# Four low parts of every gate/up chunk formed by accumulating transfers instead of VectorE, in a two-layer decoder trunk

## The chip, the core and the metric

The kernel runs on one core of one Trainium2 chip. The metric is the time of the whole program on the device in microseconds, so less is better. The core's engines run side by side and meet only at semaphores: TensorE (PE) multiplies, VectorE (DVE) and ScalarE (ACT) work elementwise, GpSimd (POOL) and SyncE (SP) here mostly start transfers (DMA).

## What is computed

A residual stream x of 256 tokens by 2048 channels, float32, goes through two layers. Each has a mixer (a gated spatial mixer in the first, attention in the second) and a feed forward part. The change lies in the feed forward parts alone:

```python
D_MODEL = 2048
SEQ = 256
D_FF = -(-8 * D_MODEL // (3 * 256)) * 256      # 5632
...
def swiglu_ffn(x, norm_g, w_gate, w_up, w_down):
    h = rms_norm(x, norm_g)
    return (jax.nn.silu(h @ w_gate) * (h @ w_up)) @ w_down
...
        x = x + swiglu_ffn(x, ffn_norm[layer], ffn_w_gate[layer], ffn_w_up[layer], ffn_w_down[layer])
```

## The kernel before

**Two parts for each number.** TensorE multiplies in a reduced float format (fp32r). So every float32 weight is split into a high part (rounded to that format) and a low part (what is left), and the activations too; a product is three matmuls: high with high, low with high, high with low (`products`, lines 1609 to 1611). All of them have 512 columns. Each weight tile is loaded from HBM into `raw`, ACT writes the high part (`w_hi`, line 741), DVE the low part as raw minus high (`w_lo`, line 1160), and TensorE uses both.

**Chunks, half groups, pairs.** The 5632 hidden columns of a layer are eleven chunks of 512, c = 0 to 10. A chunk needs the products of the activations with 2048 rows of the gate weights (g) and as many of the up weights (u). The rows are cut in eight steps of 256, numbered 0 to 7. Steps 4 to 7 of g and u are plain: one such step is a **half group**, 12 matmuls (`plain_group`). Steps 0 to 3 are done for g and u together as **pairs** s0 to s3, in a form that needs seven block products, 21 matmuls, where two half groups need 24 (`pair`). A pair asks more of DVE: three sums from the raw tile (`pair_sums`, lines 1149, 1152, 1155), and three low parts (`pair_lo`, lines 1165, 1168, 1171) behind three high parts of ACT (`pair_hi`, line 730). Chunk 0 of a layer has an order of its own ("first"); the other ten are of kind "chunk". Behind chunks 3, 7 and 10 comes the down projection of the hidden columns made so far ("down" blocks), with half groups and pairs of the same kind.

**What sets the order.** No scheduler: every engine's order is written by hand as a list of such items, and semaphores alone hold the engines together. For a "chunk" PE and DVE go in the order of `ORDERS`, ACT by a list of its own:

```python
"chunk": items("g4 g5 g6 s0 g7 s1 u4 s2 u5 s3 u6 u7"),
...
    ACT_ORDERS = {"chunk": items("g4 g5 g6 g7 s0 s1 u4 s2 u5 s3 u6 u7")}
```

Between the items each engine does what belongs to the chunk before: ACT reads one bank behind g5 (line 764), applies silu behind g6 (line 770) and writes the high part of the hidden tile behind s0 (line 609); DVE sums the banks behind g5 (lines 1183 to 1191) and behind g6 (1200, 1207), then makes the sums of s0; behind s0 comes the hidden tile's low part (983), behind g7, u4 and u5 the sums of s1, s2 and s3. PE transposes the hidden tile behind g5 (line 1516).

**Buffers.** `w_hi` and `w_lo` are rings of four half groups: ACT may write half group m when PE has used half group m - 4. A pair has one buffer, of which each third is written again when PE has used it (`s_used`). `raw` has four slots of two half groups or one pair; the loads of a chunk are g4 g5, g6 g7, s0, s1, u4 u5, s2, s3, u6 u7, and SP starts a load when every reader of what the slot held is done (`slot_free`), in this order.

**The way that the table ADDED switches.** The code has a second way to make a low part. For a half group named in `ADDED`, ACT writes the high part and then, with a second instruction, minus the high part into `w_lo` (line 743); POOL starts a transfer that adds the raw tile onto it (`add_raw`, line 541), 512 KB, from SBUF to SBUF, and PE waits for its landing (`lo_added`) in place of DVE's signal. The raw slot is free for the next load when that transfer has landed. In the kernel before, `ADDED` is empty for every kind of block, so no instruction of this way is issued.

```python
                ins = nc.scalar.activation(w_hi[:, m % RING, :, :], src, ACT.Copy)
                if m in ADDED_HG:
                    nc.scalar.activation(w_lo[:, m % RING, :, :], src, ACT.Copy, scale=-1.0).then_inc(neg_ready, 1)
...
                        pool.dma_start(w_lo[:, m % RING, :, :].bitcast(F32), raw[:, slot, half * HG:(half + 1) * HG, :],
                                       accum_op=ALU.add).then_inc(lo_added[m % RING], 16)
```

The functions that read the changed tables, with their line numbers in the profile:

Of the kernel before, what the change touches and what calls it, by code (L numbers as in the profile page):

```python
# [49 lines left out]
def yoco_kernel(nc, x, a_norm, a_w_in, a_ln_g, a_ln_b, a_w_s, a_b_s, a_w_out, kv_norm, w_k, w_v, k_norm,  # L50
# [27 lines left out]
    def items(text):  # L78
        return [(w[0], int(w[1:])) for w in text.split()]
# [16 lines left out]

    ADDED = {"chunk": [], "first": [], "down 0": [], "down 1": [], "down middle": []}


    ACT_ORDERS = {"chunk": items("g4 g5 g6 g7 s0 s1 u4 s2 u5 s3 u6 u7")}

    def kind(k):

        if k[1] == "chunk":
            return "chunk" if k[2] else "first"
        return f"down {k[3]}"

    def order(k):  # L110
        return ORDERS[kind(k)]

    def loads(k):
        return LOADS[kind(k)]
# [15 lines left out]
    for layer in range(2):  # L130
        reads = SLOT_READ[layer]
        reads += [[("half group", hg - 6 + 2 * n)] for n in range(RAW)]
        for p, (c0, c1) in enumerate(PARTS):
# [5 lines left out]
            for k in blocks:  # L139
# [11 lines left out]
                for item in order(k):  # L151
# [3 lines left out]
                    else:  # L155
                        HG_OF[k, item] = hg
                        if item in ADDED[kind(k)]:
                            ADDED_HG.append(hg)
                        hg += 1
                LAST_PAIR[k], END_OF[k] = n_pair - 1, hg  # L160
                for load in loads(k):
                    slot = len(reads) % RAW
                    n_both[slot] += len({m for m, _ in load}) > 1 or load[0][0] == "s"
                    for item in load:
                        LOAD_OF[k, item], BOTH_OF[k, item] = len(reads) - RAW, n_both[slot]
                    reads.append([("pair", PAIR_OF[k, item[1]] + 1) if item[0] == "s" else
                                  ("added", HG_OF[k, item]) if item in ADDED[kind(k)] else
                                  ("half group", HG_OF[k, item] + 1) for item in load])
# [22 lines left out]
    def in_slot(load):  # L191

        return load % RAW, load // RAW + 1
# [22 lines left out]
    with ExitStack() as ctx:  # L216
# [274 lines left out]
        def _(pool):  # L491
# [40 lines left out]
            def add_raw(layer):  # L532
                for k in (k for k in NUMBER if k[0] == layer):
                    for item in order(k):
                        if item not in ADDED[kind(k)]:
                            continue
# [22 lines left out]
        def _(act):  # L559
# [197 lines left out]
            def feed_forward(layer, norm, last_save, last_lhs):  # L757
# [18 lines left out]
                def block_hi(k, hooks):  # L776
                    for item in ACT_ORDERS.get(kind(k), order(k)):
                        slot, count = in_slot(LOAD_OF[k, item])
                        both = BOTH_OF[k, item]
                        if item[0] == "s":  # L780
                            pair_hi(PAIR_OF[k, item[1]], slot, both, before + count)
                        else:
                            load, = [w for w in loads(k) if item in w]
                            half = load.index(item)
                            if half == 0 and load[1][0] != item[0]:
                                plain_hi(HG_OF[k, item], slot, half, s_landed[slot], both)
                            else:
                                plain_hi(HG_OF[k, item], slot, half, raw_landed[slot], before + count)
                        for work in hooks.get(item, ()):
                            work()  # L790
# [158 lines left out]
        def _(dve):  # L949
# [213 lines left out]
            def pair_lo(n, slot):  # L1163
                dve.wait_ge(s_cast, n * 3 + 1)
                nc.vector.tensor_tensor(s_lo[:, 0:3, :], raw[:, slot, 1:4, :], s_hi[:, 0:3, :].bitcast(F32), ALU.subtract)\  # L1165
                    .then_inc(blocks_split, 1)
                dve.wait_ge(s_cast, n * 3 + 2)
                nc.vector.tensor_tensor(s_lo[:, 5:7, :], sums_b[:, 2:4, :], s_hi[:, 5:7, :].bitcast(F32), ALU.subtract)\  # L1168
                    .then_inc(t24_split, 1)
                dve.wait_ge(s_cast, n * 3 + 3)  # L1170
                nc.vector.tensor_tensor(s_lo[:, 3:5, :], sums_b[:, 0:2, :], s_hi[:, 3:5, :].bitcast(F32), ALU.subtract)\  # L1171
                    .then_inc(s_split, 1)

            def feed_forward(layer, norm, first_hooks):
# [74 lines left out]
                def block_lo(k, hooks):  # L1249
                    for item in order(k):  # L1250
                        slot, _ = in_slot(LOAD_OF[k, item])
                        if item[0] == "s":
                            pair_lo(PAIR_OF[k, item[1]], slot)
                        elif item not in ADDED[kind(k)]:
                            load, = [w for w in loads(k) if item in w]
# [616 lines left out]
```

## Time and profile before

| | |
|---|---|
| time, median of 3 runs | 2097.47 us (2097.42 to 2097.56) |
| the profiled execution, its own time | 2096.73 us |
| its span in the profile | 2094.6 us |
| TensorE busy | 2076.8 us, 99% of the span |
| VectorE busy | 1731.5 us, 83% |
| ScalarE busy | 1150.4 us, 55% |
| GpSimd busy | 41.9 us, 2% |
| TensorE clock granted | 1.00 |
| HBM read | 399.56 MB, 192 GB/s over the span |

The ends of matmuls are modelled in this profile, and a matmul is put down as 389 ns though the next one starts 227 ns behind it. So PE can look busy while it loses up to some 160 ns between two matmuls. Its losses are read from the starts in the timeline, from the idle time of its weight loads (PEld), and from the length of equal pieces of the program.

### The profile page before, as it was taken

The page shows a single profiled execution, that of the slowest core. Times are in us where ns is not written, and L with a number is a line of the kernel's source. Part 1 is how long each engine was busy: PE and PEld are TensorE (multiplying, and loading weights), DVE is VectorE, ACT ScalarE, POOL GpSimd, SP SyncE. Part 2 cuts the span into 40 slices and gives each one's busy share as a digit, 9 for nine tenths or more (in the row PEclk, how much of TensorE's full clock was granted, in tenths as well). Part 3 has the DMA queues.
Part 4 walks back from the last instruction along what each step waited for, and adds up shares of the span by engine and source line. Part 5 has one row for each costly group of instructions (what it writes and reads, how often), then busy time and mean ns, then how long its engine had stood idle before and what let it go on. Part 6 is the DMA issues. An engine that isn't in the chain of part 4 may idle for free.

```text
span 2094.6 us, 24421 instructions
## 1 busy us (share of the span) xinstructions
PE 2076.8 (99%) x9394; PEld 1709.2 (82%) x9394; DVE 1731.5 (83%) x1907; ACT 1150.4 (55%) x1392; POOL 41.9 (2%) x47
## 2 busy tenths in 40 slices
PE   9999999999999999999999999999999999999999
PEld 8888888888888888888888888878888888888887
DVE  5466579999899998998566666589999899988997
ACT  6444555555455554556666655465555455554553
POOL 1000000000000000000011001000000000000000
PEclk9999999999999999999999999999999999999999
DMA  8655545656465664555554454545556464665554
GB/s 327 207 174 177 181 155 208 220 187 215 160 223 181 215 209 173 207 181 202 198 184 162 159 181 166 173 154 203 209 199 205 171 224 166 221 216 175 193 191 151
DMA packets 203614, 403.19 MB, mean 192 GB/s; under 512 B 8080, under 2 KB 8688, under 8 KB 203248
## 3 DMA queue, kind: packets, MB, share of 16 engines
q1 hardware_dynamic: 202720, 398.50, 55.1%
q0 software_dynamic: 784, 3.19, 0.4%
q8 instruction: 74, 1.21, 0.2%
q14 instruction: 36, 0.29, 0.0%
HBM read 399.56 MB, written 2.10 MB: 192 GB/s over the span
## 4 chain that ended last, share of the span: by engine, by line
PE 63%; DVE 33%; issue 3%; ACT 1%; DMA 0%; SPq 0%; DVEq 0%; ACTq 0%
PE acc L1468 10%; PE acc L1472 10%; PE acc L1470 10%; PE acc L1609 9%; PE acc L1610 9%; PE acc L1611 9%; DVE w_lo L1160 6%; DVE s_lo L1165 5%; DVE sums_b L1149 4%; DVE s_lo L1168 3%; DVE sums_b L1152 2%; DVE sums_b L1155 2%; DVE s_lo L1171 2%; DVE sums_b L1191 1%; DVE stage L1187 1%
## 5 line engine op out<-in xcount | busy, mean ns | idle before, releaser
L741 ACT ACTIVATE w_hi<-raw 128x1024 fp32r<-128x1024 f32 x320 | 326.5, 1051 | 165.4 <-PE acc L1611 151.0
L1160 DVE TENSOR_TENSOR w_lo<-raw,w_hi 128x1024 fp32r<-128x1024 f32 x320 | 380.8, 1217 | 21.2 <-ACT w_hi L741 21.2
L730 ACT ACTIVATE s_hi<-sums_b 128x1024 fp32r<-128x1024 f32 x208 | 209.4, 1053 | 236.5 <-DVE sums_b L1155 235.6
L1609 PE MATMUL acc<-w_hi,a_hi 128*128 128x512 f32 x736 | 288.1, 391 | 1.3 <-DVE w_lo L1160 1.3
L1611 PE MATMUL acc<-w_hi,a_lo 128*128 128x512 f32 x736 | 286.6, 389 | 0.0
L1610 PE MATMUL acc<-w_lo,a_hi 128*128 128x512 f32 x736 | 286.4, 389 | 0.0
L1468 PE MATMUL acc<-w_hi,a_hi 128*128 128x512 f32 x640 | 254.6, 398 | 0.4 <-DVE a_lo L987 0.4
L961 DVE TENSOR_TENSOR w_lo<-raw,w_hi 128x1024 fp32r<-128x1024 f32 x127 | 154.8, 1236 | 116.7 <-ACT w_hi L579 116.6
L1472 PE MATMUL acc<-w_hi,a_lo 128*128 128x512 f32 x640 | 249.6, 390 | 0.0
L1470 PE MATMUL acc<-w_lo,a_hi 128*128 128x512 f32 x640 | 249.2, 389 | 0.0
L730 ACT ACTIVATE s_hi<-raw 128x1536 fp32r<-128x1536 f32 x104 | 154.6, 1486 | 114.1 <-PE acc L1611 114.1
L965 DVE SCALAR_TENSOR_TENSOR w_lo<-raw,gains,w_hi 128x512 fp32r<-128x512 f32 x192 | 134.4, 747 | 83.9 <-ACT w_hi L583 83.8
L579 ACT ACTIVATE w_hi<-raw 128x1024 fp32r<-128x1024 f32 x127 | 132.2, 1058 | 117.5 <-PE acc L1472 115.7
L1165 DVE TENSOR_TENSOR s_lo<-raw,s_hi 128x1536 fp32r<-128x1536 f32 x104 | 182.1, 1751 | 2.2 <-ACT s_hi L730 2.2
L1609 PE MATMUL acc<-w_hi,h_hi 128*128 128x512 f32 x448 | 174.7, 390 | 0.0
L1611 PE MATMUL acc<-w_hi,h_lo 128*128 128x512 f32 x448 | 174.3, 389 | 0.0
L1610 PE MATMUL acc<-w_lo,h_hi 128*128 128x512 f32 x448 | 174.3, 389 | 0.0
L1609 PEld LDWEIGHTS acc<-w_hi,a_hi 128*128 128x128 f32 x736 | 138.2, 188 | 29.7 <-issue 1.7
L1611 PEld LDWEIGHTS acc<-w_hi,a_lo 128*128 128x128 f32 x736 | 138.1, 188 | 28.9
L1610 PEld LDWEIGHTS acc<-w_lo,a_hi 128*128 128x128 f32 x736 | 138.2, 188 | 28.1
L583 ACT ACTIVATE w_hi<-raw,gains 128x512 fp32r<-128x512 f32 x192 | 126.2, 714 | 60.5 <-PE acc L1472 60.4
L1472 PEld LDWEIGHTS acc<-w_hi,a_lo 128*128 128x128 f32 x640 | 120.1, 188 | 25.6
(223 smaller groups left out, 3793.8 us busy)
## 6 DMA issues: line engine op xcount, KB each, us to landing
raw<-in_ffn_w_down_dram SPq DMA_DIRECT2D x68, 1024.0 KB, 5.0
raw<-in_ffn_w_gate_dram SPq DMA_DIRECT2D x46, 1024.0 KB, 5.8
raw<-in_ffn_w_up_dram SPq DMA_DIRECT2D x46, 1024.0 KB, 5.0
raw<-in_ffn_w_gate_dram SPq DMA_DIRECT2D x84, 512.0 KB, 3.8
raw<-in_ffn_w_up_dram SPq DMA_DIRECT2D x84, 512.0 KB, 5.1
raw<-in_a_w_in_dram SPq DMA_DIRECT2D x30, 1024.0 KB, 5.3
raw<-in_ffn_w_down_dram SPq DMA_DIRECT2D x40, 512.0 KB, 4.8
raw<-in_a_w_out_dram SPq DMA_DIRECT2D x16, 1024.0 KB, 4.9
```

Of the source, the lines that this page charges most:

```text
L730: nc.scalar.activation(s_hi[:, operands, :], src, ACT.Copy).then_inc(s_cast, 1)
L741: ins = nc.scalar.activation(w_hi[:, m % RING, :, :], src, ACT.Copy)
L961: nc.vector.tensor_tensor(lo, src, hi, ALU.subtract).then_inc(lo_split, 1)
L965: ins = nc.vector.scalar_tensor_tensor(out=lo[:, k, :], in0=src[:, k, :], scalar=gains[:, gain + kb:gain + kb + 1], in1=hi[:, k, :], op0=A ...
L1160: nc.vector.tensor_tensor(w_lo[:, m % RING, :, :], raw[:, slot, half * HG:(half + 1) * HG, :], w_hi[:, m % RING, :, :].bitcast(F32), ALU.s ...
L1165: nc.vector.tensor_tensor(s_lo[:, 0:3, :], raw[:, slot, 1:4, :], s_hi[:, 0:3, :].bitcast(F32), ALU.subtract)\
L1468: nc.tensor.matmul(acc[s][t][:, :], hi[:, kb, tok], w_hi[:, slot, k, :], start=kb == 0, stop=False)
L1470: nc.tensor.matmul(acc[s][t][:, :], hi[:, kb, tok], w_lo[:, slot, k, :], start=False, stop=False)
L1472: ins = nc.tensor.matmul(acc[s][t][:, :], lo[:, kb, tok], w_hi[:, slot, k, :], start=False, stop=kb == HG * n - 1)
L1609: nc.tensor.matmul(bank[:, :], hi, rhs_hi, start=start, stop=False)
L1610: nc.tensor.matmul(bank[:, :], hi, rhs_lo, start=False, stop=False)
L1611: return nc.tensor.matmul(bank[:, :], lo, rhs_hi, start=False, stop=stop)
```

## The change

Two tables change and nothing else. In a block of kind "chunk" (chunks 1 to 10 of both layers, 20 blocks) the half groups g7, u4, u5 and u7 get their low parts by the accumulating transfer. ACT's order moves too: u4 and u5 each stand one pair earlier, u7 stands ahead of s3, and u6 is last.

```diff
-    ADDED = {"chunk": [], "first": [], "down 0": [], "down 1": [], "down middle": []}
+    ADDED = {"chunk": items("g7 u4 u5 u7"), "first": [], "down 0": [], "down 1": [], "down middle": []}
...
-    ACT_ORDERS = {"chunk": items("g4 g5 g6 g7 s0 s1 u4 s2 u5 s3 u6 u7")}
+    ACT_ORDERS = {"chunk": items("g4 g5 g6 g7 s0 u4 s1 u5 s2 u7 s3 u6")}
```

The orders of PE and SP are the same row for row. On ACT, from g7 (the high part that follows the silu) to the first part of s1, before:

```order
L770 ACTIVATE stage<-stage,rstd 128x512 x2
L741 ACTIVATE w_hi<-raw 128x1024
L730 ACTIVATE s_hi<-raw 128x1536
L730 ACTIVATE s_hi<-sums_b 128x1024 x2
L609 ACTIVATE h_hi<-tr 128x512 x2
L730 ACTIVATE s_hi<-raw 128x1536
```

and now:

```order
L770 ACTIVATE stage<-stage,rstd 128x512 x2
L741 ACTIVATE w_hi<-raw 128x1024
L743 ACTIVATE w_lo<-raw 128x1024
L730 ACTIVATE s_hi<-raw 128x1536
L730 ACTIVATE s_hi<-sums_b 128x1024 x2
L609 ACTIVATE h_hi<-tr 128x512 x2
L741 ACTIVATE w_hi<-raw 128x1024
L743 ACTIVATE w_lo<-raw 128x1024
L730 ACTIVATE s_hi<-raw 128x1536
```

So g7 has a second write behind it, and the two of u4 stand between the hidden tile and s1. On DVE, from the hidden tile's low part to the sums of s2, before:

```order
L983 TENSOR_TENSOR h_lo<-tr,h_hi 128x512 x2
L1160 TENSOR_TENSOR w_lo<-raw,w_hi 128x1024
L1149 TENSOR_TENSOR sums_b<-raw 128x1024
L1152 TENSOR_TENSOR sums_b<-sums_b,raw 128x512
L1155 TENSOR_TENSOR sums_b<-sums_b,raw 128x512
L1165 TENSOR_TENSOR s_lo<-raw,s_hi 128x1536
L1168 TENSOR_TENSOR s_lo<-sums_b,s_hi 128x1024
L1171 TENSOR_TENSOR s_lo<-sums_b,s_hi 128x1024
L1160 TENSOR_TENSOR w_lo<-raw,w_hi 128x1024
L1149 TENSOR_TENSOR sums_b<-raw 128x1024
```

and now:

```order
L983 TENSOR_TENSOR h_lo<-tr,h_hi 128x512 x2
L1149 TENSOR_TENSOR sums_b<-raw 128x1024
L1152 TENSOR_TENSOR sums_b<-sums_b,raw 128x512
L1155 TENSOR_TENSOR sums_b<-sums_b,raw 128x512
L1165 TENSOR_TENSOR s_lo<-raw,s_hi 128x1536
L1168 TENSOR_TENSOR s_lo<-sums_b,s_hi 128x1024
L1171 TENSOR_TENSOR s_lo<-sums_b,s_hi 128x1024
L1149 TENSOR_TENSOR sums_b<-raw 128x1024
```

The low parts of g7 and u4 are gone from DVE, and those of u5 and u7 further on. POOL, which issued nothing in the chunks, gets one run of transfers for each layer:

```order
L541 DMA w_lo<-raw 128x1024 x40
```

It stands between the small norm steps of the two layers; nothing else was or is due on POOL inside the chunks.

## Rows read from the trace of the kernel before

**Rows 1.** Page, part 1: busy us, share of the span, count of instructions

```profile
PE 2076.8 (99%) x9394; PEld 1709.2 (82%) x9394; DVE 1731.5 (83%) x1907; ACT 1150.4 (55%) x1392; POOL 41.9 (2%) x47
```

**Rows 2.** Windows from transpose to transpose, layer 0: into chunks 2, 3 and down

```profile
core 0: us, PE busy (x) PEld busy (x) DVE busy (x) ACT busy (x) POOL busy (x), PEclk, DMA share, GB/s
336.80:378.73 41.93, 41.93 (x190) 34.48 (x189) 41.45 (x41) 24.50 (x25) 0.00 (x0) 1.00 0.58 201
378.73:421.60 42.87, 42.34 (x189) 34.38 (x188) 42.36 (x42) 24.50 (x25) 0.00 (x0) 1.00 0.56 196
421.60:464.47 42.87, 42.38 (x190) 34.39 (x189) 42.42 (x42) 24.19 (x25) 0.00 (x0) 1.00 0.56 196
```

**Rows 3.** Waits of the weight loads, whole span: us in total, times, longest

```profile
PEld acc L1609 <- DVE s_lo L1165: 29.2, 57, 1.1
```

**Rows 4.** Timeline of PE, chunk 6 of layer 0, into s1 and s2 (start, length)

```profile
602.78 0.39 PE L1611 MATMUL acc<-w_hi,a_lo 128*128 128x512 f32 x1
603.64 0.50 PE L1609 MATMUL acc<-s_hi,a_hi 128*128 128x512 f32 x1 [0.47 <-DVE s_lo L1165]
603.98 0.40 PE L1610 MATMUL acc<-s_lo,a_hi 128*128 128x512 f32 x1
...
611.03 0.39 PE L1611 MATMUL acc<-w_hi,a_lo 128*128 128x512 f32 x1
611.30 0.50 PE L1609 MATMUL acc<-s_hi,a_hi 128*128 128x512 f32 x1
611.64 0.39 PE L1610 MATMUL acc<-s_lo,a_hi 128*128 128x512 f32 x1
```

**Rows 5.** Timeline of PE, chunk 4 (the one behind a down block), into s1

```profile
559.65 0.39 PE L1611 MATMUL acc<-w_hi,a_lo 128*128 128x512 f32 x1
560.76 0.50 PE L1609 MATMUL acc<-s_hi,a_hi 128*128 128x512 f32 x1 [0.73 <-DVE s_lo L1165]
```

**Rows 6.** Timeline of DVE, chunk 6: g7, sums and low part of s1, then on

```profile
598.11 1.22 DVE L1160 TENSOR_TENSOR w_lo<-raw,w_hi 128x1024 fp32r<-128x1024 f32 x1
599.24 1.22 DVE L1149 TENSOR_TENSOR sums_b<-raw 128x1024 f32<-128x1024 f32 x1
...
601.84 1.75 DVE L1165 TENSOR_TENSOR s_lo<-raw,s_hi 128x1536 fp32r<-128x1536 f32 x1
...
606.91 1.21 DVE L1149 TENSOR_TENSOR sums_b<-raw 128x1024 f32<-128x1024 f32 x1
...
621.10 4.62 DVE L1160 TENSOR_TENSOR w_lo<-raw,w_hi 128x1024 fp32r<-128x1024 f32 x4
```

**Rows 7.** Timeline of ACT, chunk 6 and the start of chunk 7

```profile
595.01 1.06 ACT L609 ACTIVATE h_hi<-tr 128x512 fp32r<-128x512 f32 x2
597.85 1.49 ACT L730 ACTIVATE s_hi<-raw 128x1536 fp32r<-128x1536 f32 x1 [1.78 <-PE acc L1611]
...
624.06 0.60 ACT L764 ACTIVATE sums_b<-acc 128x512 f32<-128x512 f32 x1 [0.98 <-PE tr L1611]
...
629.58 1.04 ACT L741 ACTIVATE w_hi<-raw 128x1024 fp32r<-128x1024 f32 x1
```

**Rows 8.** Timeline of SP, chunk 6: the load of u6 u7

```profile
605.89 0.37 SPq L428 DMA_DIRECT2D raw<-in_ffn_w_up_dram  x1
```

**Rows 9.** Page, part 6: transfers, KB each, median us from issue to landing

```profile
raw<-in_ffn_w_up_dram SPq DMA_DIRECT2D x46, 1024.0 KB, 5.0
raw<-in_ffn_w_gate_dram SPq DMA_DIRECT2D x84, 512.0 KB, 3.8
```

**Rows 10.** The same view over the first 60 us: POOL's large transfers

```profile
w_s_nat<-in_a_w_s_dram POOLq DMA_DIRECT2D x1, 1024.0 KB, 8.2
...
ln_bias<-in_a_ln_b_dram POOLq DMA_DIRECT2D x1, 1024.0 KB, 13.8
```

**Rows 11.** Timeline of POOL: how long the issues took it

```profile
37.09 1.25 POOL L514 DMA_DIRECT2D w_s_nat<-in_a_w_s_dram  x1
38.35 0.56 POOL L515 DMA_DIRECT2D ln_gain<-in_a_ln_g_dram  x1
```

## The prediction, made before the changed kernel had run

> **What bounds the kernel now.** I read the page's first part, then the windows chunk by chunk, then the timeline where PE loses time. PE is busy 99% of the span, DVE 83% [rows 1]: at first sight TensorE is the bound and relief on DVE is worth nothing. The windows say where that is not so. From transpose to transpose a chunk takes 42.87 us, in which DVE is busy for 42.36 and 42.42 us, while the piece into chunk 2, with the same work of PE and DVE a little ahead, takes 41.93 [rows 2]. ACT has 24.5 us of work in it. So inside the chunks DVE is as full as PE, and PE waits for it a little.
>
> How: PE's weight loads waited for line 1165, the first low part of a pair, 57 times, 29.2 us [rows 3] (that sum holds the usual gaps between loads too, so it is not yet the loss). Of the 57, 54 are three (s1, s2, s3) in each of 18 chunks; chunk 1 of the two layers has the other three. Two matmuls normally start 227 ns apart. Into s1 of chunk 6 they start at 602.78 and 603.64, 0.63 us late, and the next only at 603.98, 0.11 us late again, as its weights could not be loaded ahead. Into s2 the two losses are 0.27 - 0.227 = 0.04 and 0.34 - 0.227 = 0.11 [rows 4], into s3 the same. Why 0.04 each time: between s1 and s2 DVE's own round, from one L1149 to the next, is 606.91 - 599.24 = 7.67 us [rows 6], and PE's is 21 + 12 matmuls of 227 ns, 7.48. PE is held back to DVE's pace.
>
> **What the change removes.** The loss in a usual chunk is 0.63 + 0.11 + 2 x 0.15 = 1.04 by rows 4; by the windows it is 42.87 - 41.93 = 0.94, plus the one wait of about 0.15 that chunk 1 has itself, 1.09 [rows 2]. I take 1.07. In a chunk behind a down block the wait into s1 is 560.76 - 559.65 - 0.23 = 0.88 [rows 5], so 1.3 in all. Sum: 14 x 1.07 + 4 x 1.3 + 3 x 0.15 = 15.0 + 5.2 + 0.4 = 20.6 us.
>
> DVE is rid of four instructions of 1.22 us in a chunk, started 1.13 us apart (598.11 and 599.24 in rows 6): 4 x 1.13 = 4.5 us of DVE, against a loss of about 1.1. Over 20 chunks that is 80 instructions and 90 us off DVE. Is it off at the right place? For s1, yes twice. g7's low part stands directly ahead of the sums of s1, so these and the low part behind them come 1.13 us sooner. And DVE starts the chunk's bank sums sooner: now a run of four low parts ends at 625.72 [rows 6], although ACT's read of the bank, which they also need, is done at 624.66 [rows 7]. With u7 gone they follow ACT, some 0.9 us sooner. s1 was 0.63 late and would be 1.4 us early. Behind a down block only the first of the two helps: 0.88 late becomes 0.25 early. For s2 and s3 DVE's round falls to 7.67 - 1.13 = 6.5 us against PE's 7.48, so its lead grows. All four gaps close, and the 0.11 behind each with them. What is late next is nothing within a microsecond in a usual chunk: PE runs at its own pace.
>
> **What it adds on ACT.** Four more writes (minus the high part), each about as w_hi, 1.04 us [rows 7]: 4.2 us onto 24.5 of 42.87 [rows 2]. Where each lies: g7's second write stands ahead of s0's high parts, which end up waiting for DVE's sums anyway. The two of u4 now stand between the hidden tile, done at 596.07, and s1: they end at about 598.1, where s1's first part now starts at 597.85, released by PE [rows 7]. That costs 0.3 us at most, out of the 1.4. u5 lies likewise between s1 and s2, where ACT idled about as long as before. u7 ahead of s3 needs its load landed: SP issues u6 u7 at 605.89 [rows 8], behind DVE's last part of s1, and 1 MB lands 5.0 us later [rows 9], at 610.9, or 2 us sooner if s1 is. s2's high parts on ACT are done at about 609. So ACT may idle there until 610 or so, and u7's pair ends near 612; s3's first part is due when PE has used a third of s2, near 613. No cost. u6, last, is done long before PE's turn.
>
> **What it adds in transfers.** 4 x 512 KB in a chunk, each issued when ACT's second write is done. The deadline is PE's turn for that half group. The nearest is u4: ready at 598.1, used when PE has gone through s1, 603.0 + 4.76 = 607.8, so 9.7 us ahead. For g7 it is about 11.6 us, for u5 and u7 over 11. The trace of before has no accumulating transfer. From below: a plain load of 512 KB lands after 3.8 us [rows 9]. From above: POOL's own transfers, twice as large, at a time when the DMA engines were nearly full, landed after 8.2 us and, the third in a row, after 13.8 [rows 10]. Issuing took POOL 0.56 to 1.25 us [rows 11], four times in 42 us. I take 6 us, an estimate between 3.8 and 8.2 since one is issued alone and is half as large: hidden, with 3 us to spare. The raw slots stay held until the landing, but this too is earlier than now: g7's slot is free at about 595 instead of behind DVE's g7 at 599.33. DMA load: the chunk's own weights keep the engines busy for a share of 0.56 at 196 GB/s, 8.4 MB [rows 2]; 2.1 MB more is 0.14, twice that if the add reads its target as well: 0.70 to 0.84. There is room, with less of it.
>
> **Sum.** 20.6 removed, 0 added: 2096.73 - 20.6 = 2076.1 for the profiled execution. The median of the three runs lies 0.74 above it, so 2076.9.
>
> **Rivals.** (1) *POOL and DVE share a way into SBUF.* If a transfer's issue holds DVE up for its 0.56 to 1.25 us [rows 11], four of them take 2.2 to 5.0 us from DVE, against 4.5 given: at the upper end nothing is gained, about 2097; at the lower end all is still gained. For it: DVE has hardly a gap in which POOL could go unseen. Against it: POOL reads no tile in an issue, and three issues near 38 us disturbed nothing that I can see. The Trainium skill, "SBUF — State Buffer", section "SBUF: two separate sides", has a rule that speaks against this change: a VectorE operation with two SBUF inputs excludes a GpSimd operation that reads SBUF, for the whole instruction, and whoever comes first holds it. All of DVE's low parts have two SBUF inputs. By it the time would be this rival's 2097 if it held for an issue, and POOL's issue would itself start up to 1.75 us late; no run shows it for a transfer that is only issued.
>
> (2) *The accumulating transfer is slow* (the one that ends slower). If landing takes L us, u4 is late by L - 9.7, in 20 chunks, while 20.6 is won. The sides are even at L = 10.7. At 13.8, the slowest that POOL's transfers showed [rows 10], it is 4.1 x 20 - 20.6 = 61 us slower, 2158. For it: adding reads twice and writes once, and four such transfers share the engines with loads that come in bursts. Against it: half the size of those in rows 10, and alone in the queue.
>
> (3) *A part only.* Loads crowded by the adds land later, so ACT writes u7 and then s3 late, or the chunks behind a down block keep their waits since only 0.25 us is to spare there. With one wait of 0.3 to 0.5 us left in each chunk, 6 to 10 us stay: 2083 to 2087.
>
> (4) *The tables move nothing*: excluded, as the built order shows DVE without the rows.
>
> **How the numbers follow.** Full gain, 2075 to 2079: 0.62. Part, 2079 to 2092: 0.17. No gain by rival 1, 2093 to 2101: 0.07. Slower by rival 2: 0.14. The range runs from 2075.0 (the sum with the losses taken 10% higher) to 2098.0, and leaves out rival 2 with little else. 0.2% is 4.2 us, about what a measurement of this kernel can tell from no change. Faster 0.79, same 0.07, slower 0.14.
>
> **What would show it.** Right: PE's weight loads no longer wait for line 1165, a chunk from transpose to transpose is 41.8 us in all 20, DVE shows idle time in the chunks, some 4 us each, ahead of the bank sums and of the pairs, and L1160 counts 240 in place of 320. The landing of w_lo<-raw is 4 to 8 us. Wrong: PE waits for w_lo<-raw by DMA ahead of u4 (rival 2), DVE's 1.22 and 1.75 us grow or gaps open while POOL issues (rival 1), or PE waits stay at s3 or behind down blocks (rival 3). A landing above 9.7 us alone would overturn the sign.

## The result: 2105.4 us, slower by 0.37%

| | before | changed |
|---|---|---|
| median, 20 runs each | 2097.43 us | 2105.37 us |
| lowest to highest | 2097.05 to 2098.55 | 2097.48 to 2112.85 (19 runs) |
| ratio to before, 95% interval | | 1.0037 (1.0028 to 1.0045) |
| profiled execution, its span | 2094.6 us | 2100.8 us |

The forecast was 2076.9, 20.6 us faster. One of the 20 runs of the changed kernel took 5993 us; there is no trace of it, the comparison leaves it out, and nothing below explains it. The others spread over 15 us where before they spread over 1.5. The traced run took 2102.49 us, so it shows a little less than the usual loss.

Page of the changed kernel, part 1 and part 3 (queue, packets, MB, share of 16 engines), against [rows 1]:

```profile
PE 2075.0 (99%) x9394; PEld 1711.9 (81%) x9394; DVE 1648.5 (78%) x1827; ACT 1223.2 (58%) x1472; POOL 110.5 (5%) x127
...
q1 hardware_dynamic: 202720, 398.50, 57.1%
q0 software_dynamic: 12304, 45.14, 10.5%
```

DVE is rid of 83 us and 80 instructions (90 us were forecast), ACT has 73 us more (84). The chunks, again from transpose to transpose, the same pieces as in [rows 2], and further on the pieces into chunk 7 and into the down block behind it:

```profile
core 0: us, PE busy (x) PEld busy (x) DVE busy (x) ACT busy (x) POOL busy (x), PEclk, DMA share, GB/s
336.86:379.55 42.69, 42.02 (x190) 34.53 (x189) 38.27 (x38) 28.18 (x29) 3.46 (x4) 1.00 0.89 251
379.55:422.60 43.05, 42.01 (x190) 34.53 (x189) 38.28 (x38) 28.18 (x29) 3.44 (x4) 1.00 0.83 244
422.60:464.33 41.73, 41.73 (x190) 34.62 (x189) 37.46 (x37) 27.15 (x28) 2.59 (x3) 1.00 0.83 244
...
633.82:676.63 42.81, 42.44 (x190) 34.34 (x189) 38.18 (x38) 28.06 (x29) 3.44 (x4) 1.00 0.84 246
676.63:720.23 43.60, 42.46 (x190) 34.36 (x189) 38.21 (x38) 26.68 (x28) 2.59 (x3) 1.00 0.82 237
```

The forecast was 41.8 us for each. Of the 16 such pieces of the trace two have 41.7; six, of 42.1 to 42.8, keep a part of the gain; eight are longer than before. The worst one, from 1991.5 us on, takes 46.19 in place of 42.87. DVE now has 2.8 to 7.6 us without work in each, so DVE's pace is no longer the matter. Who waits for whom (us in total, times, longest), against [rows 3]:

```profile
ACT w_hi L741 <- DMA raw<-in_ffn_w_gate_dram: 57.3, 16, 6.6
ACT w_hi L741 <- DMA raw<-in_ffn_w_up_dram: 51.7, 20, 5.9
...
PEld acc L1609 <- DVE stage L1187: 12.6, 10, 2.7
PEld acc L1609 <- DVE s_lo L1165: 11.6, 14, 2.6
```

The 54 regular waits of PE for DVE are gone. In their place ACT waits for weight loads, 36 times for 109 us, where the kernel before waited 2.3 us in all for such loads; and PE waits 24 times, for up to 2.7 us: ahead of g4 for DVE's bank sums (L1187) and ahead of a pair for its low part (L1165). PE waits for a landing of `w_lo<-raw` by itself only 0.2 us in the whole span, so the deadline that the prediction watched is met. The transfers (KB each, median us from issue to landing), against [rows 9]:

```profile
raw<-in_ffn_w_gate_dram SPq DMA_DIRECT2D x46, 1024.0 KB, 8.1
raw<-in_ffn_w_up_dram SPq DMA_DIRECT2D x46, 1024.0 KB, 6.5
...
w_lo<-raw POOLq DMA_DIRECT2D x80, 512.0 KB, 8.6
```

The loss has two places in a chunk. **Place 1**, chunk 2 of layer 0, into s3. Timelines of SP, POOL, ACT, DVE and PE:

```profile
391.45 0.37 SPq L428 DMA_DIRECT2D raw<-in_ffn_w_up_dram  x1
...
391.72 0.85 POOL L541 DMA_DIRECT2D w_lo<-raw  x1 [5.90 <-ACT w_lo L743]
...
401.53 1.06 ACT L741 ACTIVATE w_hi<-raw 128x1024 fp32r<-128x1024 f32 x1 [4.91 <-DMA raw<-in_ffn_w_up_dram]
402.50 1.04 ACT L743 ACTIVATE w_lo<-raw 128x1024 fp32r<-128x1024 f32 x1
403.44 1.47 ACT L730 ACTIVATE s_hi<-raw 128x1536 fp32r<-128x1536 f32 x1
...
404.95 1.76 DVE L1165 TENSOR_TENSOR s_lo<-raw,s_hi 128x1536 fp32r<-128x1536 f32 x1 [3.77 <-ACT s_hi L730]
...
405.33 0.39 PE L1611 MATMUL acc<-w_hi,a_lo 128*128 128x512 f32 x1
406.76 0.50 PE L1609 MATMUL acc<-s_hi,a_hi 128*128 128x512 f32 x1 [1.04 <-DVE s_lo L1165]
```

SP issues the load of u6 u7, and 0.3 us later POOL issues the transfer of u5. The load needs 10.1 us, where in the same chunk of the kernel before it needed 4.9. ACT stands at u7, which the new order puts ahead of s3, so s3 is late on ACT, then on DVE, then on PE, by 1.2 us. In the trace this load needs 9.7 to 10.7 us in five of the 20 chunks, and PE is late by 0.8 us or more at s3 in just these five; in the other 15 it lands after 6.1 to 7.6 us although u5's transfer follows it as closely. The five differ from the rest in u4's transfer: there it still had 2.6 us or more to its landing when the load was issued (here it landed at 394.06), elsewhere 2.1 us or less. The two go together in the trace; that the one is the cause of the other is not shown.

**Place 2**, from the end of chunk 4 to that of chunk 5. (The prediction and its rows call the stretch from 590 to 625 us chunk 6. It is chunk 5: its s1 starts at 603.64, one chunk of 42.88 us behind the 560.76 of chunk 4.) The chain that released each step (start, length):

```profile
561.96 8.43 DMA w_lo<-raw
570.46 9.35 DMA raw<-in_ffn_w_gate_dram
579.83 1.07 ACT w_hi L741
...
584.64 1.24 DVE stage L1187
...
604.22 0.95 ACT w_lo L743
605.17 0.28 issue
605.46 8.66 DMA w_lo<-raw
614.15 0.03 issue
614.18 7.90 DMA raw<-in_ffn_w_gate_dram
```

and what PE lost by it:

```profile
585.92 0.50 PE L1609 MATMUL acc<-w_hi,a_hi 128*128 128x512 f32 x1 [0.91 <-DVE stage L1187]
```

The transfer of u5 lands after 8.43 us; only then is the raw slot of u4 u5 free, and only then does SP load g4 g5 of the next chunk, with g6 g7 in line behind. POOL has just issued u7's transfer (570.23). The load takes 9.35 us. ACT then has to write g4 and g5, DVE their low parts, and the bank sums come behind these in DVE's order, so PE starts g4 of chunk 5 1.1 us late (the matmul ahead of it starts at 584.63). In the kernel before SP issued this load later, at 571.85, but it landed after 5.6 us.

The chain then goes on through DVE and ACT to u5's transfer of chunk 5, and PE is no part of it. So it is a **loop**, and its length is the pace of the chunks as soon as it is longer than PE's own 41.7 us. From the landing of the load of g4 g5 to the issue of the next u5 transfer it takes 25.7 us in ten of the 14 chunks that follow another chunk (27.4 to 28.4 in the four behind a chunk that lost time at place 1); 0.06 us lie between u5's landing and the load. The next round is 25.7 + 8.66 + 7.90 = 42.3 us, and from 605.46 to the next u5 transfer, at 647.73, it is just that. PE stays in front only if the landing of u5's transfer and the load behind it together need less than 41.7 - 25.7 = 16.0 us; in the change they need 15.1 to 19.2, in the median 16.8. In 14 of the 20 chunks the chain that ended last goes through u5's transfer.

### The profile page after: what moved, and what is told of

It reads as the page before. It is cut to its first block, busy times and chain, and to the rows that moved or that the text cites. A ratio compares the mean times of both kernels' runs of the same rounds, so it can differ in the third digit from the quotient of the medians.

```text
span 2100.8 us, 24501 instructions
## 1 busy us (share of the span) xinstructions
PE 2075.0 (99%) x9394; PEld 1711.9 (81%) x9394; DVE 1648.5 (78%) x1827; ACT 1223.2 (58%) x1472; POOL 110.5 (5%) x127
## 3 DMA queue, kind: packets, MB, share of 16 engines
q0 software_dynamic: 12304, 45.14, 10.5%
## 4 chain that ended last, share of the span: by engine, by line
PE 62%; DVE 17%; DMA 14%; ACT 4%; issue 3%; SPq 0%; DVEq 0%; ACTq 0%
PE acc L1468 10%; PE acc L1472 10%; PE acc L1470 10%; PE acc L1609 9%; PE acc L1611 8%; PE acc L1610 8%; DMA w_lo<-raw 6%; DMA raw<-in_ffn_w_gate_dram 4%; DVE s_lo L1165 2%; DVE sums_b L1149 2%; DMA raw<-in_ffn_w_down_dram 2%; DVE w_lo L1160 2%; DMA raw<-in_ffn_w_up_dram 1%; ACT w_hi L741 1%; DVE stage L1187 1%
## 5 line engine op out<-in xcount | busy, mean ns | idle before, releaser
L1160 DVE TENSOR_TENSOR w_lo<-raw,w_hi 128x1024 fp32r<-128x1024 f32 x240 | 286.6, 1219 | 76.6 <-ACT w_hi L741 76.3
L1609 PE MATMUL acc<-w_hi,a_hi 128*128 128x512 f32 x736 | 289.0, 393 | 8.8 <-DVE stage L1187 7.3
L1611 PE MATMUL acc<-w_hi,a_lo 128*128 128x512 f32 x736 | 286.7, 390 | 0.0
L961 DVE TENSOR_TENSOR w_lo<-raw,w_hi 128x1024 fp32r<-128x1024 f32 x127 | 154.8, 1236 | 116.6 <-ACT w_hi L579 116.5
L1165 DVE TENSOR_TENSOR s_lo<-raw,s_hi 128x1536 fp32r<-128x1536 f32 x104 | 182.3, 1753 | 32.5 <-ACT s_hi L730 32.5
L1609 PE MATMUL acc<-w_hi,h_hi 128*128 128x512 f32 x448 | 175.1, 391 | 1.3 <-DVE stage L1187 1.1
L1611 PE MATMUL acc<-w_hi,h_lo 128*128 128x512 f32 x448 | 174.4, 389 | 0.0
L1609 PEld LDWEIGHTS acc<-w_hi,a_hi 128*128 128x128 f32 x736 | 138.2, 188 | 40.3 <-DVE stage L1187 10.0
L1611 PEld LDWEIGHTS acc<-w_hi,a_lo 128*128 128x128 f32 x736 | 138.1, 188 | 29.0
```

The costliest lines, as they stand in the source:

```text
L961: nc.vector.tensor_tensor(lo, src, hi, ALU.subtract).then_inc(lo_split, 1)
L1160: nc.vector.tensor_tensor(w_lo[:, m % RING, :, :], raw[:, slot, half * HG:(half + 1) * HG, :], w_hi[:, m % RING, :, :].bitcast(F32), ALU.s ...
L1609: nc.tensor.matmul(bank[:, :], hi, rhs_hi, start=start, stop=False)
L1611: return nc.tensor.matmul(bank[:, :], lo, rhs_hi, start=False, stop=stop)
```

## Experiments

All runs have a comparison with the kernel before on the same chip, of 2097.2 to 2097.7 us. Where the edit is to the changed kernel, the diff is against it.

### Is it the transfers at all? Without them, and with small ones

```diff
-                        pool.dma_start(w_lo[...], raw[...], accum_op=ALU.add).then_inc(lo_added[m % RING], 16)
+                        continue
...
-                        sp.wait_ge(lo_added[count % RING], 16 * n_added(count))
+                        sp.wait_ge(neg_ready, n_neg(count))
```

(and PE in the same way)

> The changed kernel with its 80 accumulating transfers left out: ACT still writes minus the high part into w_lo, and PE and the raw slots wait for that write instead of a landing (so these low parts stay without their raw half; everything else is computed). Theory A, the transfers' bytes crowd the DMA engines and the weight loads land late: all new stalls go with them, 1 MB loads land in 5 to 6 us again, and the predicted gain appears, 2075 to 2079 us. Theory B, ACT's second writes and its new order hold up the pairs: most of the loss stays, 2095 to 2110. Theory C, POOL's issues disturb DVE: as A, since the issues go too.

2074.51 us, ratio 0.9892 (0.9875 to 0.9908).

```diff
-                        pool.dma_start(w_lo[:, m % RING, :, :].bitcast(F32), raw[:, slot, half * HG:(half + 1) * HG, :],
+                        pool.dma_start(w_lo[:, m % RING, 0, 0:P].bitcast(F32), raw[:, slot, half * HG, 0:P],
```

> The changed kernel with each accumulating transfer cut to the first 128 of the 1024 columns, 64 KB in place of 512 (so only these columns get the raw part added). Issues, waits and semaphores are all still there. Theory A (bytes crowd the loads): loads land in 5 to 6 us, 2075 to 2080 us. Theory C (the issues themselves, or the mere chain of ACT write, POOL issue, landing, raw slot free) : half or more of the loss stays, above 2088.

2074.37 us, 0.9892 (0.9875 to 0.9908). So the relief of DVE is worth 22.7 us, ACT's second writes and its order cost nothing, and neither do 80 issues on POOL, which take it 0.86 us each at this size as at the full one: with theories B and C gone, rival 1 of the prediction falls. DVE's instructions are as long as before also in the changed kernel, 1219 and 1753 ns against 1217 and 1751. So nothing of the exclusion between VectorE and GpSimd that the Trainium skill describes ("SBUF — State Buffer", section "SBUF: two separate sides") was to be seen for transfers that POOL only issues.

### Bytes beside the loads, or the held slot?

In this kernel the four transfers keep their size, but read `w_hi`, so the raw slots are free as soon as ACT has written.

```diff
-                        pool.dma_start(w_lo[:, m % RING, :, :].bitcast(F32), raw[:, slot, half * HG:(half + 1) * HG, :],
+                        pool.dma_start(w_lo[:, m % RING, :, :].bitcast(F32), w_hi[:, m % RING, :, :].bitcast(F32),
...
-                        sp.wait_ge(lo_added[count % RING], 16 * n_added(count))
+                        sp.wait_ge(neg_ready, n_neg(count))
```

> All four transfers with all their 512 KB, but each adds from w_hi of the same half group instead of from raw (so these low parts are wrong: minus high plus high), and SP therefore frees the raw slot as soon as ACT has written, not at the landing. PE still waits for the landing. Theory A (bytes crowd the loads): loads still land late, 2095 to 2110 us. Theory D (what hurts is that the raw slot is held 8.6 us until the transfer lands, so the next load starts late): 2074 to 2080.

2075.26 us, 0.9896 (0.9879 to 0.9912), and this with transfers as slow and loads of g slower still:

```profile
raw<-in_ffn_w_gate_dram SPq DMA_DIRECT2D x46, 1024.0 KB, 10.0
raw<-in_ffn_w_up_dram SPq DMA_DIRECT2D x46, 1024.0 KB, 6.5
...
w_lo<-w_hi POOLq DMA_DIRECT2D x80, 512.0 KB, 8.5
```

Theory A alone, which I had held first, is refuted: loads that take 10 us do no harm if they are issued early enough. SP's timeline shows by how much: the load of g4 g5 behind chunk 2 is issued right behind that of u6 u7, at 391.28, where the changed kernel issues it at 402.21. The raw slot that is held until the landing matters. Place 1 is gone too: the load of u6 u7 lands after 5.1 to 7.5 us here, though u5's transfer runs beside it and u7 stands ahead of s3. But a held slot alone is not it either:

### Shorter transfers that still hold their slots

```diff
-                                       accum_op=ALU.add).then_inc(lo_added[m % RING], 16)
+                                       ).then_inc(lo_added[m % RING], 16)
```

> All four transfers, same source, target and bytes, but plain copies instead of adds (so w_lo holds the raw values). A packet of 4096 bytes takes 328 ns as an add and 171 to 174 ns in POOL's plain transfers. If the time that the add keeps an engine is what crowds the loads: landing falls from 8.6 to 5 to 7 us, and the kernel to 2076 to 2090. If only the number of bytes or the path through POOL counts: as the change, 2098 to 2110.

2074.36 us, 0.9891 (0.9874 to 0.9907). Page, part 3:

```profile
q0 software_dynamic: 12304, 45.14, 5.4%
```

And the 80 transfers by their destination, `w_lo`:

```profile
DMA to landing us min/median/max: 2.8/6.7/8.9
```

The same packets and bytes as plain copies take 5.4% of the engines' time in place of 10.5%; less 0.4% for the other transfers of that queue, 5.0 against 10.1: **an adding transfer keeps the engines twice as long as a copying one.** The landing falls from 8.6 to 6.7 us in the median, and the load of g4 g5 behind it lands after 5.8 us in place of 8.2. In the loop of place 2 the two together need 12.7 us in place of 16.8: under the 16.0 that PE leaves, and the loss is gone.

```diff
-                        pool.dma_start(w_lo[:, m % RING, :, :].bitcast(F32), raw[:, slot, half * HG:(half + 1) * HG, :],
+                        pool.dma_start(w_lo[:, m % RING, 0, :].bitcast(F32), raw[:, slot, half * HG, :],
```

> All four transfers, each cut to its first half, 256 KB (so half of the columns' low parts stay without their raw part). Theory A (crowding by engine time): landing about 5 to 6.5 us, PE waits nearly gone, 2074 to 2082 us, as the slack is some 2 us. If the loss went with the bytes in proportion, it would be halfway: about 2088.

2074.70 us, 0.9892 (0.9875 to 0.9908), landing 6.7 us too, landing and load together 12.6. The loss is not in proportion to the bytes: it begins where the loop becomes longer than PE's work, and the changed kernel, with 16.8 against 16.0, lies just past that. This fits its spread from run to run, but only one run of it is traced.

### Which slot, which transfer

u5's transfer alone reads `w_hi` and frees its slot early:

```diff
+                    elif what == "added" and ADDED_HG.index(count) % 4 == 2:
+                        sp.wait_ge(neg_ready, n_neg(count))
                     elif what == "added":
...
+                        src = w_hi[:, m % RING, :, :].bitcast(F32) if item == ("u", 5) else \
+                            raw[:, slot, half * HG:(half + 1) * HG, :]
```

> The changed kernel, but the transfer of u5 alone adds from w_hi in place of raw, full size (so u5's low part is wrong), and the raw slot of u4 u5 is free as soon as u4's transfer has landed and ACT has written u5. All transfers run with all their bytes. Theory D1 (u5's landing holds the slot into which g4 g5 of the next chunk must be loaded, and g6 g7 queue behind it on SP): most of the 30 us come back, 2075 to 2082. Theory D2 (the loss needs u7's or g7's slot): 2095 to 2108.

2081.39 us (2078.75 to 2082.22), 0.992 (0.9904 to 0.9937). u5's slot is out of the loop; the waits for L1187, place 2, are gone, and place 1 is what is left:

```profile
PEld acc L1613 <- DVE s_lo L1169: 7.9, 6, 2.2
...
ACT w_hi L745 <- DMA raw<-in_ffn_w_up_dram: 52.3, 20, 5.6
ACT w_hi L745 <- DMA raw<-in_ffn_w_gate_dram: 3.2, 2, 1.6
```

(The edit adds four lines, so L1169 here is L1165 elsewhere.) The same edit for u7, index 3 in place of 2:

> The same for u7 alone: its transfer adds from w_hi, full size, and its raw slot is free as soon as ACT has written. Theory D1: as the change, 2098 to 2110, since u5 still holds its slot. Theory D2: 2075 to 2085.

2105.00 us (2101.62 to 2109.92, 9 runs), 1.0034 (1.0024 to 1.0044): as the change. It is u5's slot, then, and not u7's. Yet u5's transfer in its slot does no harm when u7 has none:

```diff
-    ADDED = {"chunk": items("g7 u4 u5 u7"), ...}
+    ADDED = {"chunk": items("g7 u4 u5"), ...}
...
-    ACT_ORDERS = {"chunk": items("g4 g5 g6 g7 s0 u4 s1 u5 s2 u7 s3 u6")}
+    ACT_ORDERS = {"chunk": items("g4 g5 g6 g7 s0 u4 s1 u5 s2 s3 u6 u7")}
```

> Three transfers, g7, u4, u5; u7's low part on DVE again and u7 last on ACT. Theory D1: u5 still holds its slot, but no transfer of u7 shares the engines with the loads of g4 g5 and g6 g7: a good part of the loss stays, 2080 to 2100. If only four at once are too many: 2074 to 2077.

2074.33 us, 0.9892 (0.9876 to 0.9909). My expectation leaned to the loss staying; it did not. u5's transfer lands as late as in the change (8.8 us in the median), but the load behind it now lands after 5.2: together 14.2 in this trace, under 16.0. With g7, u4 and u7 instead, in the order of the change:

> Three transfers, g7, u4, u7; u5's low part on DVE, ACT's order as in the change. Theory D1: no transfer holds the slot of u4 u5 late, so 2074 to 2080 although three transfers run. If the load of u6 u7 ahead of s3 on ACT is what hurts: 2085 to 2105.

2075.77 us, 0.9896 (0.9879 to 0.9912). Here u7 stands ahead of s3 too, but the load of u6 u7 lands after 5.1 us in the median and 6.9 at most, as no transfer of u5 runs beside it. So place 1 needs u5's transfer and u7's place ahead of s3; the run whose transfers read `w_hi` had both and no place 1, so the two alone do not make it.

### Bytes of u7, or its place in ACT's order

u7's transfer cut to 64 KB, the rest as in the change:

```diff
+                        part = (slice(0, 1), slice(0, P)) if item == ("u", 7) else (slice(0, HG), slice(0, CH))
...
```

> The change with the transfer of u7 alone cut to 64 KB (so most of u7's low part stays without its raw half); the other three full, ACT's order as in the change. If the loss has two places, (1) u5's transfer delays the load of u6 u7, for which ACT waits ahead of s3, and (2) u7's transfer delays the loads of g4 g5 that u5's held slot has already made late: place 1 stays and place 2 goes, 2079 to 2084. If place 2 is u5's held slot alone: 2095 to 2108. If both places need u7's bytes: 2074 to 2076.

2081.78 us (2080.67 to 2087.23), 0.9932 (0.9916 to 0.9949): place 2 is gone, place 1 is there with 7.9 us in 6 waits, as in the run with u5's slot freed early. So place 2 takes both: u5's slot freed late, and u7's bytes beside the loads that follow. Without these the load of g4 g5 lands after 5.9 us, and the two terms of the loop need 14.8. The same with u7 behind s3:

> The same, with u7 behind s3 in ACT's order, so nothing on ACT waits for the load of u6 u7 ahead of s3. By the two places neither is left: 2074 to 2076. If the order matters for nothing: as the run with u7 small in the change's order.

2079.72 us (2078.35 to 2081.65), 0.9913 (0.9896 to 0.9929), not the 2074 to 2076 that I expected. Place 1 is gone, as said, but a third one opens, in the waits of PE's weight loads (the edit adds two lines, so L1611 here is L1609 elsewhere):

```profile
PEld acc L1611 <- DMA w_lo<-raw: 8.3, 10, 1.5
```

Behind s3, u7's transfer is issued so late that PE waits for its landing, even at 64 KB. At full size this is the largest loss of all:

```diff
-    ACT_ORDERS = {"chunk": items("g4 g5 g6 g7 s0 u4 s1 u5 s2 u7 s3 u6")}
+    ACT_ORDERS = {"chunk": items("g4 g5 g6 g7 s0 u4 s1 u5 s2 s3 u6 u7")}
```

> All four transfers as in the change, but ACT takes u7 and u6 behind s3 in the old order, so a late load of u6 u7 no longer stands ahead of s3. Theory A1, the waits into s3 come from that place on ACT: they vanish, those ahead of the next chunk stay or grow by up to 1 us, since u7's transfer is now issued some 3 us later: 2088 to 2100 us. If the load itself is what counts wherever it stands: about as the change, 2102 to 2108.

2131.75 us (2123.45 to 2132.77), 1.0154 (1.0132 to 1.0176). The same row of the same view:

```profile
PEld acc L1609 <- DMA w_lo<-raw: 45.5, 20, 4.7
```

I had reckoned with 2088 to 2100, since I did not price u7's own deadline. The granted clock was 0.993 over this span, by which an estimated 15 of the 57 us above the run without transfers are PE at a lower clock, not waits. Beside u5's transfer u7 cannot win: ahead of s3 ACT waits for its load, behind s3 PE waits for its transfer. Without u5's it costs little, 2075.77 against 2074.35 with g7 and u4 alone (below).

### How much relief does DVE need?

```diff
-    ADDED = {"chunk": items("g7 u4 u5 u7"), ...}
+    ADDED = {"chunk": items("g7"), ...}
...
-    ACT_ORDERS = {"chunk": items("g4 g5 g6 g7 s0 u4 s1 u5 s2 u7 s3 u6")}
+    ACT_ORDERS = {"chunk": items("g4 g5 g6 g7 s0 s1 u4 s2 u5 s3 u6 u7")}
```

> Only g7 by an accumulating transfer, ACT in its old order. DVE is relieved of 1.13 us directly ahead of s1, where it was 0.65 us late, and its later rounds of 7.67 against 7.48 lose 0.2 us each twice, so s1 to s3 are just in time in a usual chunk and s3 or s1 a little late behind a down block. One transfer of 512 KB in a chunk, at its start. Theory A: few bytes, little crowding, 2077 to 2084 us. Theory C (issues disturb DVE by about a microsecond each): no gain, 2093 to 2098.

2075.77 us, 0.9898 (0.9881 to 0.9914). One transfer in a chunk brings nearly all, and the waits that stay are small:

```profile
PEld acc L1609 <- DVE s_lo L1165: 2.9, 12, 0.3
```

> Two transfers of 512 KB in a chunk, g7 and u4, ACT's order with u4 ahead of s1 and the rest as before. DVE is relieved of 2.3 us in a chunk. Theory A: two transfers 9 us apart early in the chunk, where only the loads of s2 and s3 are under way, crowd little: 2074 to 2078, at most 1.5 us better than g7 alone since the waits left there are 1.2 us. If every further transfer costs PE, it is slower than g7 alone, 2079 to 2090.

2074.35 us (2074.18 to 2074.66), 0.9890 (0.9874 to 0.9907). ACT's order there is "g4 g5 g6 g7 s0 u4 s1 s2 u5 s3 u6 u7". All chunks but the first are now as PE alone makes them, and DVE is still full, only no longer late:

```profile
336.80:378.50 41.70, 41.70 (x189) 34.63 (x189) 40.38 (x40) 26.39 (x27) 1.72 (x2) 1.00 0.76 232
378.50:420.20 41.70, 41.70 (x189) 34.59 (x188) 40.34 (x40) 26.40 (x27) 1.72 (x2) 1.00 0.72 226
```

This version beats both kernels: 1.1% faster than before, 31 us faster than the change, and level with the run that has no transfers at all (2074.51). The third transfer adds nothing to it (2074.33 with u5), the fourth costs 31 us.

## Why the prediction was wrong, point by point

- **The bound, right.** PE waits for DVE in the chunks, and the waits end when DVE is relieved. The sum was 20.6 us; without transfers 22.7 came back (2097.22 - 2074.51). 10% was missing: a usual chunk gives 1.17 us where I had 1.07. 41.8 us for a chunk was forecast, 41.70 measured.
- **ACT's added writes, right as to their own time** (nothing). The order was half right. "u7 ahead of s3 needs its load landed ... 1 MB lands 5.0 us later ... No cost": the load was issued as said, and landed after 10.1 us in the chunk shown, and after 6.1 or more in all, because u5's transfer runs beside it. I used the landing of a trace in which no transfer of POOL's ran beside the loads. That is place 1, some 7 us: 2081.4 and 2081.8 in the two runs that have it alone, against 2074.4.
- **The landing of the adding transfer: 6 us estimated, 8.6 measured** (4.4 to 10.4), above the 8.2 that I had as the upper end for it. PE's deadline of 9.7 us held all the same (u4's slowest landing took 9.7), so rival 2 as I priced it did not decide. As copies the same transfers landed in 6.7 us. The size was wrong since an add takes twice the engines' time of a copy; this I had left open in the engines' share (0.70 to 0.84; 0.82 to 0.89 in the pieces shown), but not in the landing.
- **The step that failed** is "hidden, with 3 us to spare. The raw slots stay held until the landing, but this too is earlier than now: g7's slot is free at about 595". It put the held slots at nothing, and it asked only when a slot is free, for one slot of three, and not how long the load behind it takes. For g7's slot it is true. The slot of u4 u5 was free at 605.46 + 8.66 = 614.1, hardly sooner than by DVE's old 614.66, and for a chunk that was to be a microsecond shorter; u7's transfer then slowed the load behind it (8.2 us in the median, 5.9 with u7 cut to 64 KB). That is place 2, about 23 us: the changed kernel's 2105 against 2081.4 with that slot free. Looking at this slot with my own numbers would not have shown it: with a landing of 6 us and a load of 5.0 the loop is 25.7 + 11.0 = 36.7 us, with 5 us to spare (an estimate from the change's own trace). Nor would either size alone: 8.8 + 5.0 and 6 + 8.2 (medians of the traced run) both stay below 16.0. It took the loop and both sizes as they were measured.
- **The rivals.** Rival 1 was refuted. Rival 3 named the mechanism, "loads crowded by the adds land later, so ACT writes u7 and then s3 late", and priced it at 6 to 10 us: right for place 1 (7). None of them has place 2: rival 3 stops at a part of the gain, and rival 2 has PE wait for the landing itself, which it did for 0.2 us in all. Rival 4 stayed excluded: L1160 counts 240. The range ended at 2098 because only rival 2 could make the kernel slower.

What stays open: the run of 5993 us; whether it is u4's transfer, still under way, that makes the load of u6 u7 need 10 us in some chunks and 6 to 8 in the others; and what sets the landing of u5's transfer and of the load behind it within their 15.1 to 19.2 us. The last decides which chunks lose at place 2, and no run varies it by itself.

## What to carry to other kernels

When work moves from an engine to transfers, list every buffer that the transfer holds until it lands, one by one, ask which load stands behind it, and follow that load on until the chain comes back to the same transfer of the next round: that loop has to be shorter than the round of the engine that you want to be the bound. Here an engine's read of the buffer ended in a microsecond, a transfer's in nine. Price the other loads at the landing they will have beside the new transfers, not at the one that they had without, above all where an in-order engine stands waiting for them ahead of something urgent. And relieve an engine by what it is late and not by what can be moved: here one of the four transfers gave 21.5 us, two 23, and all four lost 8.

## What the runs showed of the hardware that was not expected

An adding transfer within SBUF took twice the engine time of a copying one with the same packets and bytes (10.1% against 5.0% of 16 engines' span for 80 x 512 KB). The Trainium skill gives a fit for POOL's transfers, "DMA: Bandwidth & Descriptors", section "Anatomy of one DMA — SWDGE (gpsimd) path", of 2.0 us plus the bytes by 436 GB/s, by which 512 KB would be an estimated 3.2 us. The trace does not bear that out for these transfers: the one at a chunk's start, with no other of POOL's beside it, landed in 4.4 us in the median, and those of u4, u5 and u7, with loads beside them, in 6.3 to 10.4. So it is the traffic that has to be priced.

PE's two longest stops in the trace of the change are of 2.3 us each: ahead of g4 at 1942.23, after which the granted clock stayed at 1.00, and ahead of the last down block at 2030.70, right behind which it fell. Windows around the second, with the clock as the third value from the end:

```profile
2020.00:2025.00 5.00, 5.00 (x24) 4.14 (x23) 0.34 (x1) 0.39 (x1) 0.00 (x0) 1.00 1.05 326
2025.00:2031.00 6.00, 3.74 (x17) 2.81 (x16) 5.19 (x6) 3.39 (x5) 0.00 (x0) 0.95 1.05 400
2031.00:2036.00 5.00, 5.00 (x17) 3.97 (x17) 4.90 (x6) 1.97 (x3) 0.00 (x0) 0.72 0.40 157
```

0.72 is a mean of the two levels, 2.4 and 1.2 GHz, over those 5 us. What the lower level took is 0.28 of them, 1.4 us, and 0.05 of the 6 us before, 0.3 us: an estimated 1.7 us on top of a wait of 2.3.
